# Second block's three turns worked token block by token block: first projection, transposed banks and evacuation split, ScalarE in place of VectorE for block 0

## The chip, the cores and the metric

The kernel runs on one core of one Trainium2 chip. The metric is the device time of one execution in microseconds (us). The kernel before takes 2768.85 us, the median of 3 runs (2766.33 to 2769.89). Of this kernel a difference of about 0.2% (5.5 us) can be told from none. Engines: PE is TensorE (PEld its weight loads), DVE VectorE, ACT ScalarE, POOL GpSimd, SP the engine that issues most DMAs.

## The reference

256 tokens of width 1024 pass through two layers of a first block and then through a second block. The change is in the second block:

```
for i in range(DEPTH):                         # i = 0: attention (MLA), i = 1: pooling
    hx = x * (1.0 + sc1) + sh1
    y  = mla(hx) @ w_o      or   pool_mixer(hx)
    x  = layernorm(ALPHA * x + g1 * y)
    h  = x * (1.0 + sc2) + sh2
    q  = (h @ w_q).reshape(b, l, 8, 2, 128)     # PEER: 8 heads of queries
    s  = scores of q against two sets of 128 keys; top 16 of each, top 16 of the sums
    y  = sum over the chosen experts of gate * gelu(u_e . h) * v_e
    x  = layernorm(ALPHA * x + g2 * y)
```

`pool_mixer` is a projection `h @ w_in`, a windowed mean minus the value itself per group, a grouped product, a scale and `@ w_out`. All inputs are float32. The experts are not gathered: all 128 groups of 128 are computed and weighted, most of them zero.

## The kernel before

The 256 tokens are two blocks (`tb`) of 128. `x` lies in SBUF with tokens on the partitions; a product needs `h` transposed (`hT`, features on the partitions, 8 tiles `kt` of 128 features by 256 tokens). Most products are made three times from split operands (`pe_three`, L2000): a rounded high part and the remainder of weights and of `hT` (`q_high` and `ring_r` of the weights, `PX.hh`, shown as peer_pass_high, and `h_low` of the activations). ACT rounds the high parts, DVE subtracts them to give the low ones. Each engine runs its own list in written order; semaphores tie them.

Between two stages of the second block lies what this text calls a **turn**: the end of one output product, the post-norm, the transposes, and the first projection of the next stage. There are three with a next stage: **turn A** (n=0, attention to the first expert layer, near 1001 us of the span), **turn B** (n=1, first expert layer to pooling, near 1842 us) and **turn C** (n=2, pooling to the second expert layer, near 1914 us). The last post-norm (n=3) ends the kernel.

A turn before, in order. DVE (`dve_post_norm`): for each block and each half of the features a multiply by the gate, an add and the statistics (L2409 to L2411), the aggregate (L2415); POOL turns the variance into 1/sigma (L3045, L3046), DVE normalises the block (`normalise`, L2387): block 0 after the statistics of half (1, 0), block 1 at the end. PE (`pe_transpose`) transposes block 0 as soon as it is normalised, then block 1 (L1943); a bank holds two features' tiles of both blocks, so that no bank is full before block 1 is done. Idle stretches of PE are filled with products of zeros (`pe_warm`, L514). `mod_evac` copies the four banks to `hT` with scale and shift, banks 0 and 2 by ACT (L2371), 1 and 3 by DVE (L2369). Then PE runs the first projection, plain float32, 256 columns to a matmul (query 0, L2198; z 0 in turn B, L2331), while ACT makes `PX.hh` (L2949, L3021) and the high parts of the next weights (L2626, L2610) and DVE `h_low` (L2718, L2800) and the low parts (L2617, L2603). The next projections (L2000) wait for `w_low_ready`. DVE also applies the norm's own gain and shift to `x` (L2426, L2433), which only the next post-norm needs.

In an expert layer, DVE then selects (top-16 searches L2632 to L2645, gates L2692 to L2708), with the low parts of the first experts' weights dealt in between (`EarlyLows.beside`, L2581), by which PE's `early_up` products go. PE then builds the table of weights in groups (L2264) from one-hot tiles that DVE makes.

Weights come through a ring of four SBUF slots of 1 MB. SP issues the loads in order: `used(g)` waits until PE has released the slot's previous contents. The four loads of `qk1` (queries of the second expert layer) start with ring slot 0, whose previous content is the last slot of the pooling's output product.

Of the kernel before, what the change touches and what calls it, by code (L numbers as in the profile page):

```python
# [2026 lines left out]
def pe_mla(k, pe):  # L2027
# [146 lines left out]
    pe_warm(k, pe, 0, WARM_MLA[0])  # L2174


def pe_peer(k, pe, l):
# [4 lines left out]
    def query(h):
        r = STREAM.ring(f"qk{l}", h)
        if h in SPLIT_QUERIES:
            pe.wait_ge(k.w_low_ready, query_split(l, h) + l + 1)
        else:
            pe.wait_ge(k.weights_loaded[r], STREAM.loaded(f"qk{l}", h))
        b = J.give(pe, ("q", h), l)
        for kk in range(2):
            for kt in range(KT):  # L2190
                to, w = ps[b][:, kk * S:(kk + 1) * S], slice(kk * D + kt * P, kk * D + (kt + 1) * P)
                if h in SPLIT_QUERIES:
                    m = pe_three(pe, to, (k.q_high[query_high(h)][:, w], k.ring_r[r][:, w]), (k.PX.hh[:, kt, :], k.h_low[:, kt, :]),
                                 kt == 0, kt == KT - 1)
                else:
                    if h == kk == kt % 2 == 0:
                        J.evac(pe, ("xt", kt // 2), l)
                    m = pe.matmul(to, k.ring[r][:, w], k.hT[:, kt, :], start=kt == 0, stop=kt == KT - 1)  # L2198
# [112 lines left out]
def pe_pool(k, pe):  # L2311
    J, ps = k.J4, k.psum
    pe_warm(k, pe, (k.J3.at[("g", 1)] + 1) % NBANK, WARM_LATE[0])
    pe_transpose(k, pe, J, "xt", k.x, None, k.x2_done, lambda tb: k.x2_done.at(2 + tb + 1), WARM_LATE[1])
# [1 line left out]
    for i in range(4):
        if i in SPLIT_POOL:
            pe.wait_ge(k.w_low_ready, pool_split(i) + 1)
            w = k.ring_r[STREAM.ring("pool", i)]
        else:  # L2320
            w = slot(k, pe, "pool", i)
        b = J.give(pe, ("z", i))
        for kk in range(2):
            for kt in range(KT):
                to, at = ps[b][:, kk * S:(kk + 1) * S], slice(kk * D + kt * P, kk * D + (kt + 1) * P)
                if i in SPLIT_POOL:
                    m = pe_three(pe, to, (k.q_high[i][:, at], w[:, at]), (k.PX.hh[:, kt, :], k.h_low[:, kt, :]), kt == 0, kt == KT - 1)
                else:
                    if i == kk == kt % 2 == 0:
                        J.evac(pe, ("xt", kt // 2))  # L2330
                    m = pe.matmul(to, w[:, at], k.hT[:, kt, :], start=kt == 0, stop=kt == KT - 1)  # L2331
# [1104 lines left out]
```

## Time and profile before

| | us |
|---|---|
| median of 3 runs | 2768.85 |
| the profiled execution, whole time | 2765.63 |
| its span | 2763.8 |
| what lies around the span | 1.8 |
| PE busy | 2711.2 (98%) |
| DVE busy | 2110.3 (76%) |
| ACT busy | 1245.8 (45%) |
| chain that ended last: PE, DVE | 81%, 16% |

The profile is one execution, in which an engine's busy time is the union of its instructions. Matmuls overlap each other, so PE at 98% isn't PE at its peak. The chain that ended last goes back from the last instruction, at each step to what released it. In a timeline, consecutive instructions of a kind stand as one row with a count; the brackets at a row's end give the idle time of the engine before it and who ended it.

### The profile page before, as it was taken

How to read it: one execution, taken by the hardware profiler on the slowest of the kernel's cores; microseconds unless marked ns; L12 is line 12 of the kernel's file. 1: busy time of each engine (PE TensorE's matmuls, PEld its weight loads, DVE VectorE, ACT ScalarE, POOL GpSimd, SP SyncE). 2: the span in 40 equal slices, each digit the busy share in tenths (PEclk: the TensorE clock that was granted, in tenths of full speed). 3: DMA queues.
4: the chain of work that ended last, by engine and by line, in shares of the span. 5: the costliest groups of instructions: out<-in, count | busy, mean ns of one | idle time of the engine just before them, and what ended most of it. 6: DMA issues, size and time to landing. Idle time of an engine off the chain costs nothing.

```text
span 2763.8 us, 51870 instructions
## 1 busy us (share of the span) xinstructions
PE 2711.2 (98%) x20680; PEld 2370.5 (86%) x20680; DVE 2110.3 (76%) x3795; ACT 1245.8 (45%) x1878; POOL 58.9 (2%) x86
## 2 busy tenths in 40 slices
PE   9999999999999999999999999999999999999998
PEld 7887998886998679998999998876999989999886
DVE  6867887876874669999666667775999966666777
ACT  4524554433553434454444445442445444444443
POOL 0020000020000000000000000000000000000000
PEclk9999999999999999999999999999999999999999
DMA  5315884314883235643555556664564345555664
GB/s 211 107 34 218 329 319 145 121 38 182 323 332 142 72 137 191 229 155 113 184 191 187 184 194 238 242 215 151 175 232 166 128 169 186 194 182 188 238 240 171
DMA packets 87667, 515.05 MB, mean 186 GB/s; under 512 B 10192, under 2 KB 16720, under 8 KB 30672
## 3 DMA queue, kind: packets, MB, share of 16 engines
q1 hardware_dynamic: 74256, 485.11, 48.7%
q10 hardware_dynamic: 13248, 27.63, 2.8%
q8 instruction: 119, 1.95, 0.3%
q14 instruction: 44, 0.36, 0.0%
HBM read 494.88 MB, written 17.83 MB: 186 GB/s over the span
## 4 chain that ended last, share of the span: by engine, by line
PE 81%; DVE 16%; issue 1%; ACT 1%; DMA 0%; POOL 0%; ACTq 0%; DVEq 0%; SPq 0%; POOLq 0%
PE bank L907 19%; PE bank L895 19%; PE bank L934 12%; PE bank L2000 9%; DVE ring_r L2581 4%; PE bank L2264 3%; PE bank L577 2%; PE bank L726 2%; PE bank L779 2%; PE bank L2282 1%; PE bank L655 1%; DVE sb L2645 1%; DVE sb L2636 1%; PE bank L556 1%; DVE sb L2637 1%
## 5 line engine op out<-in xcount | busy, mean ns | idle before, releaser
L2000 PE MATMUL bank<-peer_pass_high,q_high 128*128 128x256 f32 x1232 | 356.4, 289 | 1.7 <-ACT sb L2935 0.9
L2000 PE MATMUL bank<-h_low,q_high 128*128 128x256 f32 x1232 | 347.7, 282 | 0.0
L2000 PE MATMUL bank<-peer_pass_high,ring_r 128*128 128x256 f32 x1232 | 347.1, 282 | 0.0
L907 PE MATMUL bank<-peer_pass_high,peer_pass_hidden 128*128 128x512 f32 x1024 | 339.5, 393 | 0.0
L895 PE MATMUL bank<-peer_pass_high 128*128 128x256 f32 x1008 | 283.2, 281 | 0.0
L895 PE MATMUL bank<-peer_pass_high,ring_r 128*128 128x256 f32 x1008 | 282.9, 281 | 0.0
L895 PE MATMUL bank<-hT_r,peer_pass_high 128*128 128x256 f32 x1008 | 282.9, 281 | 0.0
L1013 DVE TENSOR_TENSOR ring_r<-ring,peer_pass_high 128x1024 fp32r<-128x1024 f32 x128 | 156.8, 1225 | 157.8 <-ACT peer_pass_high L1646 157.8
L2000 PEld LDWEIGHTS bank<-peer_pass_high,q_high 128*128 128x128 f32 x1232 | 233.9, 190 | 2.8 <-issue 2.2
L2000 PEld LDWEIGHTS bank<-peer_pass_high,ring_r 128*128 128x128 f32 x1232 | 233.5, 190 | 0.0
L2000 PEld LDWEIGHTS bank<-h_low,q_high 128*128 128x128 f32 x1232 | 232.8, 189 | 0.0
L1646 ACT ACTIVATE peer_pass_high<-ring 128x1024 fp32r<-128x1024 f32 x128 | 135.7, 1060 | 210.7 <-DMA ring<-in_experts 209.9
L907 PEld LDWEIGHTS bank<-peer_pass_high,peer_pass_hidden 128*128 128x128 f32 x1024 | 192.5, 188 | 38.9
L1133 ACT ACTIVATE peer_pass_high<-ring 128x1024 fp32r<-128x1024 f32 x128 | 135.5, 1060 | 164.7 <-PE bank L934 164.7
L907 PE MATMUL bank<-ring_r,peer_pass_hidden 128*128 128x512 f32 x512 | 201.2, 393 | 0.0
L1666 ACT ACTIVATE sb<-bank 128x256 f32<-128x256 f32 x192 | 73.9, 385 | 273.4 <-PE bank L895 267.9
L895 PEld LDWEIGHTS bank<-peer_pass_high 128*128 128x128 f32 x1008 | 190.0, 188 | 5.8
L895 PEld LDWEIGHTS bank<-hT_r,peer_pass_high 128*128 128x128 f32 x1008 | 190.1, 189 | 5.2
L895 PEld LDWEIGHTS bank<-peer_pass_high,ring_r 128*128 128x128 f32 x1008 | 190.0, 188 | 0.0
L907 PE MATMUL bank<-ff_high,ff_hidden 128*128 128x512 f32 x512 | 170.8, 395 | 0.8 <-DVE ff_hidden L1031 0.8
L934 PE MATMUL bank<-peer_pass_high,peer_pass_hidden 128*128 128x512 f32 x512 | 166.1, 394 | 0.9 <-DVE peer_pass_hidden L1118 0.9
L934 PE MATMUL bank<-peer_pass_high,late_hidden 128*128 128x512 f32 x512 | 165.0, 392 | 0.0
(428 smaller groups left out, 6329.4 us busy)
## 6 DMA issues: line engine op xcount, KB each, us to landing
ring<-in_experts SPq DMA_DIRECT2D x256, 1024.0 KB, 4.8
ring<-in_w SPq DMA_DIRECT2D x137, 1024.0 KB, 4.8
sb<-in_w_mod SPq DMA_DIRECT2D x48, 1024.0 KB, 6.7
sb<-spill SPq DMA_DIRECT2D x64, 256.0 KB, 4.9
spill<-sb ACTq DMA_DIRECT2D x20, 512.0 KB, 6.5
spill<-sb ACTq DMA_DIRECT2D x48, 128.0 KB, 2.3
sb<-in_ln ACTq DMA_DIRECT2D x8, 512.0 KB, 4.4
sb<-in_post ACTq DMA_DIRECT2D x4, 512.0 KB, 4.7
```

What stands on the lines that cost most here:

```text
L577: m = pe.matmul(to, w[:, cols], k.hT[:, kt, :], start=kt == 0, stop=kt == KT - 1)
L726: m = pe.matmul(ps[b][rows, h * 64:h * 64 + 64], lhsT[rows, GH * g + h, :], r, start=True, stop=True)
L895: m = pe.matmul(ps[X.banks[u]][:, 0:S], w, h[:, kt, :], start=(kt, i) == (0, 0), stop=(kt, i) == (KT - 1, 2))
L907: m = pe.matmul(ps[4 + 2 * tb + half][:, :], g[:, t], w, start=False, stop=False, skip_group_check=True)
L934: m = pe.matmul(ps[4 + 2 * tb + d][:, :], g[:, rows], w, start=False, stop=False, skip_group_check=True)
L1013: v.tensor_tensor(X.ring_r[u][:, 0:D], X.ring[u][:, 0:D], X.uh[u % 2].bitcast(F32), ALU.subtract).then_inc(X.u_split, 1)
L1133: a.activation(X.late_vh[t % 4], k.ring[r][:, half * D:(half + 1) * D], ACT.Copy).then_inc(k.late_v_high, 1)
L1646: a.activation(X.uh[u % 2], X.ring[u][:, 0:D], ACT.Copy).then_inc(X.u_high, 1)
L1666: a.activation(X.r[u % 2], k.psum[X.banks[u]][:, 0:S], func).then_inc(X.acted, 1)
L2000: m = pe.matmul(out, l, r, start=start and i == 0, stop=stop and i == 2)
L2264: m = pe.matmul(ps[g % 4][:, t * P:(t + 1) * P], k.one_hot[g % 3][:, 0, t // 2, :, t % 2], k.gate_parts[g % 2][:, i, t // 2, :, t % 2], st ...
L2581: self.v.tensor_tensor(k.ring_r[r], k.ring[r], k.q_high[early_high(s)].bitcast(F32), ALU.subtract).then_inc(k.early_low, 1)
```

## The change

The turns with n below 3 are rewritten.

- `pe_turn` replaces `pe_transpose` and the first projection. Each of the four transposed banks now holds four features' tiles of one block (`("xt", 0)` and `("xt", 1)` block 0, 2 and 3 block 1). Projection 0 is cut by block and by half of the features, 128 columns to a matmul, and the first quarter stands ahead of block 1's transposes.
- Block 0 is normalised by ACT (`act_normalise`), with a bias -mean/sigma that POOL works out in a third instruction; DVE normalises block 1 alone.
- All four banks are evacuated by ACT (`act_turn`), four instructions of 128 columns to a bank; `PX.hh` and `h_low` are made block by block.
- ACT makes the high part of the next weights (query 1, or pool slot 1) ahead of `act_normalise`; DVE makes its low part first of all after the post-norm.
- The warming products: 4 in turns A and B, ahead of the transposes; before there were 8 in A, 8 and 10 in B, 10 in C.
- `k.gate` of the expert layers moves from `hT`'s upper half to columns of `W`, and the gates are addressed as 8 x 64.
- Semaphore counts follow: `x2_first` for block 0, `hh_ready` two per turn.

```diff
-    j = [(("xt", i), both(i)) for i in range(4)]
+    j = [(("xt", i), "act") for i in range(4)]
...
+def pe_turn(k, pe, J, n, it, key, weights):
+    banks = [J.give(pe, ("xt", i), it) for i in range(4)]
+    def transposed(tb):
+        for kt in range(KT):
+            b = banks[2 * tb + kt // 4]
+            t = pe.transpose(k.psum[b][:, kt % 4 * P:(kt % 4 + 1) * P], k.x[:, tb, kt * P:(kt + 1) * P], k.c["ident"])
+            if kt % 4 == 3:
+                t.then_inc(J.filled, 1)
+    pe.wait_ge(k.x2_first, n + 1)
+    transposed(0)
+    b = J.give(pe, key, it)
+    w = weights()
+    def project(tb, half):
+        for kk in range(2):
+            for kt in range(4 * half, 4 * half + 4):
+                m = pe.matmul(k.psum[b][:, kk * S + tb * P:kk * S + (tb + 1) * P], w[:, kk * D + kt * P:kk * D + (kt + 1) * P],
+                              k.hT[:, kt, tb * P:(tb + 1) * P], start=(tb, half, kk, kt) == (0, 0, 0, 0),
+                              stop=(tb, half, kk, kt) == (1, 1, 1, KT - 1), skip_group_check=True)
+        return m
+    project(0, 0)
+    pe.wait_ge(k.x2_done.sem, k.x2_done.at(n + 1))
+    transposed(1)
+    J.evac(pe, ("xt", 1), it)
+    project(0, 1)
+    for half in range(2):
+        J.evac(pe, ("xt", 2 + half), it)
+        m = project(1, half)
+    m.then_inc(J.filled, 1)
+
+def act_normalise(k, a, n):
+    a.wait_ge(k.ln_rstd.sem, k.ln_rstd.at(2 * n + 1))
+    a.activation(k.x[:, 0, :], k.x[:, 0, :], ACT.Identity, scale=k.stat[:, 12:13], bias=k.stat[:, 0:1]).then_inc(k.x2_first, 1)
+
+def act_turn(k, a, J, it, shift, scale, high, done):
+    def evacuate(i):
+        b = J.take(a, "act", ("xt", i), it)
+        for j in range(4):
+            kt, cols = i % 2 * 4 + j, slice(i // 2 * P, (i // 2 + 1) * P)
+            m = a.activation(k.hT[:, kt, cols], k.psum[b][:, j * P:(j + 1) * P], ACT.Identity, scale=scale[:, kt:kt + 1],
+                             bias=shift[:, kt:kt + 1])
+        m.then_inc(J.read["act"], 1)
+    for tb in range(TB):
+        evacuate(2 * tb)
+        evacuate(2 * tb + 1)
+        J.evac(a, ("xt", 2 * tb + 1), it)
+        cols = slice(tb * P, (tb + 1) * P)
+        a.activation(high[:, :, cols], k.hT[:, :, cols], ACT.Copy).then_inc(done, 1)
+
+def dve_h_low(k, v, tb):
+    cols = slice(tb * P, (tb + 1) * P)
+    v.tensor_tensor(k.h_low[:, :, cols], k.hT[:, :, cols], k.PX.hh[:, :, cols].bitcast(F32), ALU.subtract).then_inc(k.w_low_ready, 1)
...
@@ dve_post_norm
-            if (tb, half) == (1, 0):
+            if (tb, half) == (1, 0) and n == 3:
                 finish(0)
...
@@ dve_peer
-    mod_evac(k, v, J, "dve", "xt", lambda kt: k.hT[:, kt, :], k.hshift[:, 2 * l, :], k.hscale[:, 2 * l, :], l)
-    dve_affine_scale(k, v, sd, J, 2 * l, l)
-    J.evac(v, ("xt", 2), l)
-    v.wait_ge(k.hh_ready, l + 1)
-    v.tensor_tensor(k.h_low, k.hT, k.PX.hh.bitcast(F32), ALU.subtract).then_inc(k.w_low_ready, 1)
     dve_query_low(k, v, l, 1)
+    v.wait_ge(k.hh_ready, 2 * l + 1)
+    dve_h_low(k, v, 0)
+    dve_affine_scale(k, v, sd, J, 2 * l, (0,), l)
+    v.wait_ge(k.hh_ready, 2 * l + 2)
+    dve_h_low(k, v, 1)
     dve_query_low(k, v, l, 2)
+    dve_affine_scale(k, v, sd, J, 2 * l, (1,), l)
     dve_affine_shift(k, v, sd)
     dve_query_low(k, v, l, 3)
...
@@ dve_pool
-    mod_evac(k, v, J, "dve", "xt", lambda kt: k.hT[:, kt, :], k.hshift[:, 1, :], k.hscale[:, 1, :])
+    dve_pool_low(k, v, 1)
+    v.wait_ge(k.w_high_ready, pool_split(1) + 1)
+    dve_h_low(k, v, 0)
     dve_diag(k, v, k.mod[:, 1, G1:G1 + 8])
...
@@ act_mla, end (and the same at the end of act_pool with 1, 1 and 2; act_pool begins with its own pair)
     act_gate_row(k, a, J, k.gbc)
+    act_query_high(k, a, 0, 1)
+    act_normalise(k, a, 0)
...
@@ pool_ln_rstd
+        if n < 3 and tb == 0:
+            sp.link(m)
+            m = p.tensor_scalar(k.stat[:, 0:1], k.mv[:, tb, 0:1], r, -1.0, ALU.mult, ALU.mult)
```

How the instructions stand. ACT in turn C, before; the first rows end the pooling stage (L2841 copies the gate row), `q_high_74` is the high part of query 1's weights, in ring slot 1:

```order
L2834 DMA sb<-in_ln 128x1024 x2
L2841 ACTIVATE sb<-bank 128x512 [waits pool_bank_filled] x2
L2371 ACTIVATE sb<-bank,sb 128x256 [waits peer_bank_filled,h_columns,x2_done]
L2371 ACTIVATE sb<-bank,sb 128x256
L2371 ACTIVATE sb<-bank,sb 128x256 [waits peer_bank_filled]
L2371 ACTIVATE sb<-bank,sb 128x256
L2949 ACTIVATE peer_pass_high<-sb 128x2048 [waits peer_bank_read_dve,peer_bank_read_act]
L2626 ACTIVATE q_high_74<-ring 128x2048 [waits weights_loaded1]
L2626 ACTIVATE q_high_75<-ring 128x2048 [waits weights_loaded2]
```

The same place of the changed kernel (L2684 is the old L2626, L1986 `act_normalise`, L1995 and L2004 `act_turn`):

```order
L2900 ACTIVATE sb<-bank 128x512 [waits pool_bank_filled] x2
L2684 ACTIVATE q_high_74<-ring 128x2048 [waits weights_loaded1]
L1986 ACTIVATE sb<-sb 128x1024 [waits ln_rstd]
L1995 ACTIVATE sb<-bank,sb 128x128 [waits peer_bank_filled,h_columns]
L1995 ACTIVATE sb<-bank,sb 128x128 x3
L1995 ACTIVATE sb<-bank,sb 128x128 [waits peer_bank_filled]
L1995 ACTIVATE sb<-bank,sb 128x128 x3
L2004 ACTIVATE peer_pass_high<-sb 128x8x128 [waits peer_bank_read_act]
L1995 ACTIVATE sb<-bank,sb 128x128 [waits peer_bank_filled]
```

The high part of query 1's weights, with its wait for the load of ring slot 1, has moved from behind the evacuation to ahead of the normalising of block 0, which itself is new on ACT.

PE in turn A, before (L514 warms, L1943 transposes, L2198 is query 0):

```order
L514 MATMUL bank<-sb 128x512 x8
L1943 MATMUL bank<-sb 128x128 [waits x2_done]
L1943 MATMUL bank<-sb 128x128 x7
L1943 MATMUL bank<-sb 128x128 [waits x2_done]
L1943 MATMUL bank<-sb 128x128 x7
L2198 MATMUL bank<-sb,ring 128x256 [waits peer_bank_read_act,weights_loaded0]
L2198 MATMUL bank<-sb,ring 128x256
L2198 MATMUL bank<-sb,ring 128x256 [waits peer_bank_read_dve]
```

And in the changed kernel (L1955 transposes, L1967 is query 0 in quarters):

```order
L514 MATMUL bank<-sb 128x512 x4
L1955 MATMUL bank<-sb 128x128 [waits x2_first]
L1955 MATMUL bank<-sb 128x128 x7
L1967 MATMUL bank<-sb,ring 128x128 [waits weights_loaded0,peer_bank_read_act]
L1967 MATMUL bank<-sb,ring 128x128 x7
L1955 MATMUL bank<-sb 128x128 [waits x2_done]
L1955 MATMUL bank<-sb 128x128 x7
L1967 MATMUL bank<-sb,ring 128x128 [waits peer_bank_read_act]
```

A quarter of query 0 has moved between the two blocks' transposes, which thereby stand behind block 0's evacuation by ACT.

## Rows read from the trace of the kernel before

**Rows 1.** The page: busy time by engine, and the chain that ended last.
```profile
PE 2711.2 (98%) x20680; PEld 2370.5 (86%) x20680; DVE 2110.3 (76%) x3795; ACT 1245.8 (45%) x1878; POOL 58.9 (2%) x86
...
PE 81%; DVE 16%; issue 1%; ACT 1%; DMA 0%; POOL 0%; ACTq 0%; DVEq 0%; SPq 0%; POOLq 0%
```

**Rows 2.** Selection: stretch, its length, busy PE, PEld, DVE, ACT, POOL, clock, DMA.
```profile
1110.00:1130.00 20.00, 20.00 (x170) 20.00 (x169) 19.79 (x76) 9.37 (x11) 0.00 (x0) 1.00 0.69 218
```

**Rows 3.** Waits: DVE 1009.5 to 1176, PE 1016.6 to 1182 (us, times, longest).
```profile
DVE sb L2443 <- DVE sb L2725: 0.2, 1, 0.2
...
PE bank L2264 <- DVE sb L2763: 1.7, 1, 1.7
```

**Rows 4.** Timeline of turn A: start, us, engine, line, instruction, count, idle before.
```profile
1000.27 0.55 POOL L3046 TENSOR_TENSOR sb<-sb 128x1 f32<-128x1 f32 x1
...
1001.76 0.80 DVE L2387 TENSOR_SCALAR sb<-sb 128x1024 f32<-128x1024 f32 x1
...
1005.81 0.81 DVE L2387 TENSOR_SCALAR sb<-sb 128x1024 f32<-128x1024 f32 x1 [0.95 <-POOL sb L3046]
...
1006.67 1.09 PE L1943 MATMUL bank<-sb 128*128 128x128 f32 x8 [2.98 <-DVE sb L2387]
1007.23 1.93 ACT L2371 ACTIVATE sb<-bank,sb 128x256 f32<-128x256 f32 x4 [28.03 <-PE bank L1943]
1007.44 1.90 DVE L2369 TENSOR_SCALAR sb<-bank,sb 128x256 f32<-128x256 f32 x4 [0.82 <-PE bank L1943]
...
1008.40 8.64 PE L2198 MATMUL bank<-sb,ring 128*128 128x256 f32 x32 [0.63 <-ACT sb L2371]
1009.26 2.35 DVE L2426 TENSOR_TENSOR sb<-sb 128x1024 f32<-128x1024 f32 x2
...
1016.68 0.47 PE L2000 MATMUL bank<-peer_pass_high,q_high 128*128 128x256 f32 x1
...
1020.52 2.29 DVE L2617 TENSOR_TENSOR ring_r<-ring,q_high 128x2048 fp32r<-128x2048 f32 x1
```

**Rows 5.** Timeline of turn B, as rows 4.
```profile
1848.52 0.64 ACTq L3017 DMA_DIRECT2D sb<-in_const  x1
...
1857.73 0.38 PE L2000 MATMUL bank<-peer_pass_high,q_high 128*128 128x256 f32 x1 [0.21 <-DVE ring_r L2603]
...
1866.68 2.28 DVE L2603 TENSOR_TENSOR ring_r<-ring,q_high 128x2048 fp32r<-128x2048 f32 x1
```

**Rows 6.** Timeline of turn C, as rows 4.
```profile
1914.02 20.39 SPq L3056 DMA_DIRECT2D ring<-in_w  x6
...
1920.23 7.14 PE L2198 MATMUL bank<-sb,ring 128*128 128x256 f32 x32 [0.63 <-ACT sb L2371]
...
1923.09 5.68 ACT L2626 ACTIVATE q_high<-ring 128x2048 fp32r<-128x2048 f32 x3
...
1927.95 0.36 PE L2000 MATMUL bank<-peer_pass_high,q_high 128*128 128x256 f32 x1 [0.57 <-issue]
...
1935.40 0.87 DVE L2632 MAX8 sb<-sb 128x8 f32<-128x128 f32 x4 [0.75 <-ACT sb L2925]
```

**Rows 7.** SP's first two loads of turn C: issues, and time to landing.
```profile
L3056 SPq DMA_DIRECT2D ring<-in_w x2: 328/380/433, 1914.0 to 1914.4; - x2
...
DMA to landing us min/median/max: 4.7/6.1/7.5
```

**Rows 8.** Groups by form: busy us, mean ns of one, idle before.
```profile
L2371 ACT ACTIVATE sb<-bank,sb 128x256 f32<-128x256 f32 x24 | 11.5, 569 | 78.3 <-PE bank L1943 78.3
L2930 ACT ACTIVATE sb<-sb 128x128 f32<-128x128 f32 x4 | 1.2, 311 | 10.3 <-DVE sb L2674 10.2
L1610 ACT ACTIVATE sb<-sb 128x1024 f32<-128x1024 f32 x3 | 3.1, 1051 | 5.4 <-DMA sb<-in_c_rows 5.4
L2209 PE MATMUL bank<-sb 128*128 128x128 f32 x128 | 16.8, 275 | 0.0
```

**Rows 9.** The same view of turn A after the transposes (0.83: granted clock).
```profile
1008.00:1018.00 10.00, 9.60 (x42) 8.40 (x43) 10.00 (x8) 9.08 (x8) 0.00 (x0) 0.83 0.15 61
```

More of the change, by code:

```diff
@@ L1844, in pool_jobs @@
 def pool_jobs():
-    j = [(("xt", i), both(i)) for i in range(4)]
+    j = [(("xt", i), "act") for i in range(4)]
     j += [(("z", i), "act") for i in range(4)]
@@ L1899, in plan_memory2 @@
     assert n.off + 4 * D <= k.mod_at + SLOT
-    k.gbc, k.lng, k.lnb, k.diag = n.take(D), n.take(D), n.take(D), n.take(8, P)
+    gbc, k.lng, k.lnb, k.diag = n.take(D), n.take(D), n.take(D), n.take(8, P)
+    k.gbc = [shaped(gbc[:, i * 512:(i + 1) * 512], 8, 64) for i in range(2)]
     k.ptmp = [k.diag.rearrange("p a b -> p (a b)")[:, i * 512:(i + 1) * 512] for i in range(2)]
@@ L2191, in query @@
                 to, w = ps[b][:, kk * S:(kk + 1) * S], slice(kk * D + kt * P, kk * D + (kt + 1) * P)
[L2192 to L2198, printed above, removed]
+                m = pe_three(pe, to, (k.q_high[query_high(h)][:, w], k.ring_r[r][:, w]), (k.PX.hh[:, kt, :], k.h_low[:, kt, :]),
+                             kt == 0, kt == KT - 1)
                 rel.pay(m) if kt == 0 else None
@@ L2312, in pe_pool @@
     J, ps = k.J4, k.psum
-    pe_warm(k, pe, (k.J3.at[("g", 1)] + 1) % NBANK, WARM_LATE[0])
-    pe_transpose(k, pe, J, "xt", k.x, None, k.x2_done, lambda tb: k.x2_done.at(2 + tb + 1), WARM_LATE[1])
+    pe_warm(k, pe, (k.J3.at[("g", 1)] + 1) % NBANK, WARM_LATE)
     rel = Release(k)
[L2316 to L2321, printed above, removed]
+    pe_turn(k, pe, J, 1, None, ("z", 0), lambda: slot(k, pe, "pool", 0))
+    rel.owe()
+    for i in SPLIT_POOL:
+        pe.wait_ge(k.w_low_ready, pool_low(i))
+        w = k.ring_r[STREAM.ring("pool", i)]
         b = J.give(pe, ("z", i))
@@ L2325, in pe_pool @@
                 to, at = ps[b][:, kk * S:(kk + 1) * S], slice(kk * D + kt * P, kk * D + (kt + 1) * P)
[L2326 to L2331, printed above, removed]
+                m = pe_three(pe, to, (k.q_high[i - 1][:, at], w[:, at]), (k.PX.hh[:, kt, :], k.h_low[:, kt, :]), kt == 0, kt == KT - 1)
                 rel.pay(m) if kt == 0 else None
@@ L2609, in act_pool_high @@
     a.wait_ge(k.weights_loaded[r], STREAM.loaded("pool", i))
-    a.activation(k.q_high[i], k.ring[r], ACT.Copy).then_inc(k.w_high_ready, 1)
+    a.activation(k.q_high[i - 1], k.ring[r], ACT.Copy).then_inc(k.w_high_ready, 1)
 def dve_query_low(k, v, l, i):
@@ L2840, in act_gate_row @@
         b = J.take(a, "act", ("g", i), it)
-        a.activation(gate[:, i * 512:(i + 1) * 512], k.psum[b][:, :], ACT.Copy).then_inc(J.read["act"], 1)
+        a.activation(gate[i], shaped(k.psum[b][:, :], 8, 64), ACT.Copy).then_inc(J.read["act"], 1)
 def act_keys(k, a, l):
@@ L2945, in early_up @@
                         k.early[:, n - 3:n + 1, :].rearrange("p a b -> p (a b)")).then_inc(k.early_out, 16)
[L2947 to L2950 removed]
+    for i in (2, 3):
         act_query_high(k, a, l, i)
@@ L3242, in build @@
         k.PX.late_gl = k.PX.gl + [spare[:, (2 + i) * S:(3 + i) * S] for i in range(2)]
-        k.gate = k.sb[:, k.hT_at + 4 * S:k.hT_at + KT * S]
+        k.gate = [k.W[:, 8 * i:8 * i + 8, 0:EXP_SLOTS] for i in range(2)]
         k.FF = Pass(k, ctx, nc, "ff", FF_SLOTS, k.ff_at, k.ff_hi, FF_RING, k.J1.at[("h2", 0)] % NBANK)
```

89 lines of the change are left out of this document (42 added, 47 removed).

## The prediction

> **What bounds the kernel now.** I read the page first: PE is busy in 98% of the span, and the chain that ended last is PE for 81% and DVE for 16% [rows 1]. So a turn matters only by when PE can go on, and where DVE's 16% lie. The stretches of the selection phase answer the second: from 1110 to 1130 PE is busy for 20.00 of 20 us and DVE for 19.79 [rows 2]. The waits complete it: from the end of turn A's evacuation to the end of the selection DVE waits 0.2 us in all, and PE 1.7 us at the first group of gates, for DVE [rows 3]. Both are full, but DVE ends last. So a turn ahead of an expert layer (A and C) is worth what it gives DVE, read at the last low part of the turn, where nothing of DVE's list can be moved: L2617 at 1020.52 in A [rows 4]. PE's gain beyond that is lost in waits for the experts' low parts. Last come the timelines of the turns [rows 4 to 6] and the landings of the loads [rows 7].
>
> **Turn A, step by step.** DVE drops the normalising of block 0 (0.80 us, about 0.7 with its overlap), so block 1's normalise moves from 1005.81 to 1005.1 and ends at 1005.9 [rows 4]. POOL's power ends at 1000.82 [rows 4]; with a third small instruction ACT can begin at 1001.25, and 128x1024 takes ACT 1.05 [rows 8]: block 0 is ready at 1002.3, before the former 1002.6. PE transposes it (1.09 for eight [rows 4]); bank 0 is full at 1003.0, ACT starts at 1003.15. What one ACT instruction of 128 columns costs isn't in the trace. Four of 256 take 1.93 with 0.569 the last, so they start 0.45 apart [rows 4, 8]. The bounds are 0.45 above (nothing saved by half the columns) and 0.25 below (0.311 for a 128x128 without a column bias [rows 8], less overlap). I take 0.35, near the middle. Eight then take 2.9. The high part of a block (half of 1.9) is 1.05.
>
> ACT: block 0 to 1006.05, its high part to 1007.2. PE: quarter (0, 0) from 1004.8. A 128-column float32 matmul counts two instructions, and the scores' 16 runs of eight take 1.05 each with 0.275 the last, so 0.111 apart [rows 8]; a quarter is 16 of them, 1.8. All four are 7.1, what 32 of 256 columns take at full clock (7.14 [rows 6]): the split costs PE nothing. Quarter (0, 0) ends at 1006.6, then come block 1's transposes, which could have started at 1006.0. ACT evacuates block 1 from 1007.4 to 1010.3, its high part is there at 1011.45. PE ends the last quarter at 1013.1 and can begin query 1, before at 1016.68 [rows 4]: 3.5 earlier.
>
> DVE: low part 1 from 1006.0 to 1008.25 (2.29 each [rows 4]), `h_low` 0 (1.2) and one scaling (1.2, half of L2426's 2.35 [rows 4]) to 1010.6. Here 0.9 of waiting is new, for ACT's high part; `h_low` 1 to 1012.7; again 0.65 of waiting, because ACT makes high part 2 only now (to 1013.3); low part 2, a scaling, two shifts, and low part 3 ends at 1021.3, before at 1022.8 (1020.52 + 2.29). DVE is relieved of 0.7, of 1.90 for the evacuation and of the wait of 0.82 [rows 4], but waits 1.6 for ACT, which now carries all. **A: -1.5**, bounds 0 (ACT at 0.45) and -3.5 (all of PE's gain counts).
>
> **Turn B.** The same, with pool slot 1 landed well ahead, since the last experts' loads end earlier. On ACT, two DMA issues (one of them 0.64, L3017 [rows 5]) now stand between block 1 and high part 2, about 1.0 in all. DVE's low part 3, which projection 3 waits for, was done at 1868.96 [rows 5]; the same sum gives 1867.25, and the pooling adds behind it fill DVE. **B: -1.7**, bounds 0 and -3.1 (PE's own: projection 1 at 1854.6 for 1857.73 [rows 5]).
>
> **Turn C.** Here one step changes sign. ACT's list has the high part of query 1 ahead of block 0's normalise, and it needs ring slot 1. SP starts all four loads of `qk1` only at 1914.02, when the output product has released its last slot; the first lands after 4.7, the second, issued at 1914.4, after 7.5: 1921.9 [rows 6, 7]. Before, ACT came to it at 1923.09 and found it there [rows 6]. Now ACT stands still from the gate row on; behind it are the normalise, all evacuations and both high parts, PE's transposes wait for the normalise, and DVE for both. Slot 1 lands at 1921.9, the high part ends at 1923.85, block 0 is normalised at 1924.9. Before, block 0 was normalised about when the output product ended, 1914. From there the sum of turn A, with nothing to hide it: ACT starts on bank 0 at 1925.75, ends block 0's high part at 1929.8, takes bank 2 at 1929.95, and ends block 1's high part at 1934.0; `h_low` 1 at 1935.25; PE begins query 1 at 1935.5, before at 1927.95 [rows 6]: +7.6. DVE: high part 2 is made by 1935.85, low part 2 to 1938.1, scaling and shifts to 1941.5, low part 3 to 1943.7, and the first search starts at 1943.9, before at 1935.40 [rows 6]: +8.5.
>
> To this comes the clock. In turn A PE waits 2.98 and 0.63 [rows 4], and then is granted 0.83 over 1008 to 1018 (the lower level, 1.2 GHz, for a third of it) [rows 9]: query 0 takes 8.64 for 7.14 [rows 4, 6]. In turn C PE now has nothing for 11 us. The lower level for the transposes alone costs 0.5 of the chain, for the first quarter too 2.1; with nothing lowered 0. I take 1.5, what query 0 lost in A. **C: +10.0**, bounds +7.6 and +12.5 (with ACT at 0.45).
>
> The Trainium skill (TensorE: Matmul & The Clock Gate, Part 1: The HAM clock gate) has the slow clock as the default, which only activity lifts; the trace agrees [rows 9]. By that rule turn C resumes at 1.2 GHz for certain; by a rule that the clock depends on the matmuls alone it wouldn't, and C were +8.5. A and B lose warming products too, but PE's gaps there shrink to about 1 us, and I set 0.
>
> At nothing: `k.gate`'s strided address (as many elements), the keys' DMA 1.4 later (needed by query 1 at 1013, behind two loads already in flight), and POOL's third instruction, which only block 0 waits for (0.3, included).
>
> **Sum:** -1.5 - 1.7 + 10.0 = +6.8. The profiled execution took 2765.63 (span 2763.8 and 1.8 around it), so 2772.4 by its own measure. It lies 3.2 under the median of the runs, 2768.85, so that what is timed should read 2775.6.
>
> **The rivals.**
> 1. *PE decides, not DVE.* Then A is -3.5, B -3.1, C +7.6 and 1.5 of clock: +2.5, 2771.4. For it: the chain is PE's in 81%, and where PE waits it waits for 1.7 only [rows 1, 3]. Against it: DVE has no gap in which to take up its part [rows 2, 3].
> 2. *Faster: ACT isn't held.* Were slot 1 there by the time ACT reaches it, C would be like A and the wait of 0.75 at L2632 [rows 6] would go too, -2.3: the sum is -5.5, 2763.3. It decides if the second load lands before about 1915. For it is only that SP might issue slot 1 earlier; against it that SP's list is unchanged and its first issue of the four is at 1914.02 [rows 6]. A partial case: both loads share the DMA engines and land together at 4.7, which makes slot 1 2.8 earlier: +4.0, 2772.9. The Trainium skill (DMA: Bandwidth & Descriptors, Queues, rings and completion order) says that completion isn't in the order of issue; here the two land 3.2 apart in order [rows 7]. By the page's rule alone the sum would be +4.0 or +6.8.
> 3. *The clock falls in all three turns.* The new PE lists alternate short work and waits of 1 us with fewer warming products. 1.5 more in A and in B, and 1 more in C: +10.8, 2779.7. For it: rows 9, after 3 us of waiting; against it: no waits of that length are left in A and B.
>
> **Numbers.** Chances: forecast 0.70, rival 1 0.13, rival 2 0.08 (with its partial case), rival 3 0.09. A difference under 0.2% (5.5 us) can't be told from none. The forecast's own range goes from 2771.5 (+2.7: gains near their bounds, no clock) to 2780 (+11); within it about a quarter lies under +5.5. Slower: 0.70 x 0.74 + 0.09 = 0.61; faster 0.05, half of rival 2 and a little; same 0.34. The range for 8 in 10 takes in most of rival 1 and of rival 3: 2769 to 2781.
>
> **What would show it.** In the changed profile: in turn C the normalise L1986 waits behind L2684, and L2684 for DMA into the ring, over 30 us of idle ACT ended by in_w; L1955 there starts near 1925 less what A and B gave (3.2), that is near 1922; PE idle for about 11 us ahead of it and the granted clock under 1 right after. In A the search starts 1.5 earlier, with two DVE waits for ACT (0.9 and 0.65), and PE waits more often for low parts. In B projection 3 waits for L2661's low part. I am wrong if L2684 in turn C is done before the output product's end, if the 128-column evacuations start 0.25 or 0.45 apart, or if the selection ends earlier than DVE's share allows.

## The result

| | median us | n | ratio to before, 95% interval |
|---|---|---|---|
| before | 2768.16 | 19 | |
| changed | 2773.5 | 19 | 1.002 [1.0013, 1.0027] |

The change makes the kernel 5.3 us slower, just under the 5.5 that were called the smallest telling difference; forecast were +6.8 and 2775.6. The interval lies above 1, so the loss is clear of the spread, though small. The profiled execution has a span of 2769.4 for 2763.8. Of all executions behind the ratios below, three were left out of them as far above the rest (2970 to 9953 us: one of experiment 8, two of the kernel before beside experiments 5 to 8); the medians include them.

The page of the changed kernel, as in [rows 1]:

```profile
PE 2705.3 (98%) x20739; PEld 2371.3 (86%) x20748; DVE 2103.7 (76%) x3783; ACT 1260.9 (46%) x1920; POOL 59.7 (2%) x89
...
PE 79%; DVE 17%; issue 2%; ACT 2%; DMA 1%; POOL 0%; DVEq 0%; ACTq 0%; SPq 0%; POOLq 0%
```

PE is busy 5.9 less and the end is 5.6 later: PE stands still somewhere. ACT and DMA, which had 1% and 0% of the chain, now have 2% and 1%.

To price each turn by itself I measure from the first `BATCH_NORM_AGGREGATE` of a turn to the first search (`MAX8`) of the expert layer behind it, or in turn B to the aggregate of turn C. So what happens outside the turns drops out.

| profile | A | B | C |
|---|---|---|---|
| before | 25.00 | 70.33 | 23.94 |
| changed | 23.37 | 67.35 | 33.86 |
| difference | -1.63 | -2.98 | +9.92 |
| forecast | -1.5 | -1.7 | +10.0 |

The three sum to +5.3, 1.5 less than the forecast's +6.8, and 1.3 of that lies in turn B. From C's first search to the last aggregate it is 822.2 in both.

Timeline of turn C of the changed kernel (columns as [rows 6]), all engines:

```profile
1907.12 0.21 DVE L2464 BATCH_NORM_AGGREGATE sb<-sb 128x2 f32<-128x12 f32 x1
...
1909.68 35.98 SPq L3118 DMA_DIRECT2D ring<-in_w  x7
...
1917.21 1.91 ACT L2684 ACTIVATE q_high<-ring 128x2048 fp32r<-128x2048 f32 x1 [35.35 <-DMA ring<-in_w]
1919.03 1.23 ACT L1986 ACTIVATE sb<-sb 128x1024 f32<-128x1024 f32 x1
...
1920.31 1.97 PE L1955 MATMUL bank<-sb 128*128 128x128 f32 x8 [10.63 <-ACT sb L1986]
1921.52 2.90 ACT L1995 ACTIVATE sb<-bank,sb 128x128 f32<-128x128 f32 x8 [1.26 <-PE bank L1955]
...
1923.07 3.55 PE L1967 MATMUL bank<-sb,ring 128*128 128x128 f32 x16 [0.80 <-ACT sb L1995]
...
1926.46 1.04 PE L1955 MATMUL bank<-sb 128*128 128x128 f32 x8
1927.09 2.90 ACT L1995 ACTIVATE sb<-bank,sb 128x128 f32<-128x128 f32 x8 [1.59 <-PE bank L1955]
...
1931.11 1.22 DVE L2010 TENSOR_TENSOR h_low<-sb,peer_pass_high 128x1024 fp32r<-128x1024 f32 x1 [3.22 <-ACT peer_pass_high L2004]
1932.91 2.29 DVE L2675 TENSOR_TENSOR ring_r<-ring,q_high 128x2048 fp32r<-128x2048 f32 x1 [0.58 <-ACT q_high L2684]
...
1938.77 2.29 DVE L2675 TENSOR_TENSOR ring_r<-ring,q_high 128x2048 fp32r<-128x2048 f32 x1
1940.98 0.86 DVE L2690 MAX8 sb<-sb 128x8 f32<-128x128 f32 x4
```

The reader is to see one row first: ACT was idle for 35.35 us and was released by the load into the ring, at 1917.21, 7.5 after SP's first issue. The chain that ended last passes through it: the second of SP's loads, from 1910.05, for 7.14 us, then this high part, the normalise and the transposes. Behind it come the normalise, PE (idle for 10.63) and DVE. Between the last low part and the search DVE has no gap, so its list still decides. The clock there, by stretches (columns as [rows 2]):

```profile
1914.00:1918.00 4.00, 0.00 (x0) 0.00 (x0) 0.00 (x0) 0.79 (x1) 0.00 (x0) 0.50 1.01 422
1918.00:1922.00 4.00, 1.69 (x8) 1.56 (x8) 1.72 (x1) 2.73 (x4) 0.00 (x0) 0.50 0.81 342
1922.00:1926.00 4.00, 3.20 (x15) 2.93 (x14) 1.04 (x2) 3.47 (x8) 0.00 (x0) 0.50 0.00 0
1926.00:1930.00 4.00, 4.00 (x36) 4.00 (x36) 1.89 (x2) 2.90 (x8) 0.00 (x0) 0.97 0.00 0
```

It fell while PE had nothing to do, and stayed at 0.50 through the transposes and the first quarter of query 0.

Turn A of the changed kernel answers to [rows 4]:

```profile
1002.64 1.24 ACT L1986 ACTIVATE sb<-sb 128x1024 f32<-128x1024 f32 x1 [4.78 <-POOL sb L3107]
...
1004.68 2.90 ACT L1995 ACTIVATE sb<-bank,sb 128x128 f32<-128x128 f32 x8 [0.81 <-PE bank L1955]
...
1006.24 2.05 PE L1967 MATMUL bank<-sb,ring 128*128 128x128 f32 x16 [1.22 <-ACT sb L1995]
...
1012.78 1.22 DVE L2010 TENSOR_TENSOR h_low<-sb,peer_pass_high 128x1024 fp32r<-128x1024 f32 x1 [0.88 <-ACT peer_pass_high L2004]
...
1014.58 2.29 DVE L2675 TENSOR_TENSOR ring_r<-ring,q_high 128x2048 fp32r<-128x2048 f32 x1 [0.58 <-ACT q_high L2684]
```

Eight small evacuations take 2.90 and DVE's two new waits for ACT are 0.88 and 0.58.

### The profile page after: what moved, and what is told of

Read it like the earlier page. It is cut to its first block, busy times and chain, and to the rows that moved or that the text cites. A ratio compares the mean times of both kernels' runs of the same rounds, so it can differ in the third digit from the quotient of the medians.

```text
span 2769.4 us, 52027 instructions
## 1 busy us (share of the span) xinstructions
PE 2705.3 (98%) x20739; PEld 2371.3 (86%) x20748; DVE 2103.7 (76%) x3783; ACT 1260.9 (46%) x1920; POOL 59.7 (2%) x89
## 4 chain that ended last, share of the span: by engine, by line
PE 79%; DVE 17%; issue 2%; ACT 2%; DMA 1%; POOL 0%; DVEq 0%; ACTq 0%; SPq 0%; POOLq 0%
PE bank L907 19%; PE bank L895 19%; PE bank L934 12%; PE bank L2064 8%; DVE ring_r L2631 3%; PE bank L2320 3%; PE bank L577 2%; PE bank L726 2%; PE bank L779 2%; PE bank L2338 1%; PE bank L2051 1%; DVE sb L2703 1%; DVE sb L2694 1%; PE bank L655 1%; DVE sb L2695 1%
## 5 line engine op out<-in xcount | busy, mean ns | idle before, releaser
L934 PE MATMUL bank<-peer_pass_high,peer_pass_hidden 128*128 128x512 f32 x512 | 166.0, 394 | 0.0
L934 PE MATMUL bank<-peer_pass_high,late_hidden 128*128 128x512 f32 x512 | 165.1, 392 | 0.0
```

The costliest lines, as they stand in the source:

```text
L934: m = pe.matmul(ps[4 + 2 * tb + d][:, :], g[:, rows], w, start=False, stop=False, skip_group_check=True)
```

## The experiments

There are twelve. Medians are of 10 to 12 executions each (experiment 12 is one execution), beside the kernel before in the same session; the three sessions had 2766.40 (experiments 1 to 4), 2767.74 (5 to 8) and 2767.08 (9 to 11) for it. Times of different sessions are compared by their distance from it; the changed kernel's is 5.3. The turns in the profile of each:

| | A | B | C | median | ratio to before, 95% interval |
|---|---|---|---|---|---|
| changed | 23.37 | 67.35 | 33.86 | 2773.50 | 1.0020 [1.0013, 1.0027] |
| 1 high part late in C | 25.02* | 67.36 | 27.56 | 2767.31 | 1.0001 [0.9992, 1.0010] |
| 2 slot order 1, 2, 0, 3 | 23.39 | 69.00* | 25.33 | 2765.35 | 0.9992 [0.9982, 1.0003] |
| 3 and transposes first | 25.02* | 67.36 | 24.97 | 2761.66 | 0.9979 [0.9970, 0.9988] |
| 4 C warmed | 25.03* | 67.35 | 33.55 | 2772.32 | 1.0018 [1.0009, 1.0027] |
| 5 less DVE in A | 20.97 | 67.36 | 34.56 | 2770.59 | 1.0011 [1.0002, 1.0020] |
| 6 less PE in A | 23.39 | 67.36 | 34.53 | 2774.50 | 1.0022 [1.0014, 1.0031] |
| 7 hold in the kernel before | 25.68 | 70.35 | 30.41 | 2773.63 | 1.0023 [1.0013, 1.0032] |
| 8 gaps warmed | 23.38 | 67.35 | 33.71 | 2772.04 | 1.0014 [1.0002, 1.0026] |
| 9 as 3, again | 23.39 | 67.35 | 24.95 | 2761.40 | 0.9978 [0.9967, 0.9989] |
| 10 slots and warming | 23.38 | 67.37 | 22.37 | 2758.76 | 0.9972 [0.9961, 0.9983] |
| 11 and DVE's waits filled | 22.12 | 67.35 | 22.26 | 2758.57 | 0.9968 [0.9956, 0.9980] |
| 12 kernel before, again | 24.99 | 70.48 | 23.94 | 2764.44 (one) | |

A star marks a turn of the new form in which the clock fell in the first quarter of projection 0, which then took 3.5 to 3.7 for 2.05. The profiles differ most where no turn is: turn A's first aggregate comes at 996.1 to 1005.0, so a difference of a few us between two profiled spans says less than the turns do.

**Is it the hold?** Experiment 1 moves the one instruction, and DVE's low part that follows from it, in turn C alone.

```diff
-    act_query_high(k, a, 1, 1)          # end of act_pool, ahead of act_normalise(k, a, 2)
...
-    for i in (2, 3):                    # act_peer, behind act_turn
+    for i in (2, 3) if l == 0 else (1, 2, 3):
...
-    dve_query_low(k, v, l, 1)           # DVE: in layer 1 behind dve_h_low(k, v, 1)
```

> The changed kernel, but in turn C alone ACT makes query 1's high part behind act_turn, with queries 2 and 3, instead of ahead of act_normalise (DVE's low part 1 stands behind h_low 1). Theory (the high part's wait for ring slot 1 holds ACT, and with it everything of the turn): the 35 us of idle ACT ended by in_w are gone from before the normalise; block 0 is normalised as soon as POOL's power is there, about when the output product ends, and PE now waits for slot 0, which lands 4.7 after its issue; turn C loses about 2 against the kernel before instead of 9.9, the whole is 7 to 8.5 faster than the changed kernel. Rival (the new order of PE's list and the eight small evacuations cost turn C most of its 9.9): the normalise comes early, but the first search of turn C stays over 6 later than before, and the whole within 3 of the changed kernel.

```profile
1907.80 1.24 ACT L1986 ACTIVATE sb<-sb 128x1024 f32<-128x1024 f32 x1 [26.91 <-POOL sb L3109]
...
1913.91 2.80 PE L1967 MATMUL bank<-sb,ring 128*128 128x128 f32 x16 [3.72 <-DMA ring<-in_w]
...
1916.50 1.91 PE L1955 MATMUL bank<-sb 128*128 128x128 f32 x8
```

Turn C lost 3.6 instead of 9.9, and the kernel is level with the one before: 4.4 less than the changed kernel, where 7 to 8.5 were expected. By turn C the hold is 6.3 of the 9.9. My 2 was too small by 1.6: PE's new wait of 3.72 for slot 0 also lets the clock fall (quarter 2.80 for 2.05, transposes 1.91 for 1.04), and block 1's transposes stand behind that quarter. Turn A of this profile had its own fall (25.02).

**The same from the other side.** Experiment 2 leaves the lists of all engines that compute and changes only SP's order of loads.

```diff
-        for pos in range(0 if seg == "mla" else RING):
+        for pos in () if seg == "mla" else (1, 2, 0, 3) if seg == "qk1" else range(RING):
```

> The changed kernel, but SP issues the four loads of qk1 in the order slot 1, 2, 0, 3; slots 1 and 2 were released earlier in the pooling, slots 0 and 3 only at the end of the output product. The other engines' lists are unchanged. Theory (only the landing of slot 1 holds ACT): the high part of query 1 is made well before the output product ends, ACT's wait for in_w goes, and turn C now waits for slot 0, 4.7 after its issue: first search of turn C 8 earlier than in the changed kernel, the whole 8 less. Partial rival (slot 0 shares the queue with two loads that are still in flight and lands later): 5 to 6 less. Rival (ACT is held by something else): nothing changes.

```profile
1912.92 1.24 ACT L1986 ACTIVATE sb<-sb 128x1024 f32<-128x1024 f32 x1 [12.81 <-POOL sb L3107]
...
1918.76 3.04 PE L1967 MATMUL bank<-sb,ring 128*128 128x128 f32 x16 [3.45 <-DMA ring<-in_w]
```

ACT now waits for POOL, not for the load, and turn C is 8.5 shorter, as expected. The median is 1.1 under the kernel before, an interval that takes in 1, and 6.4 under the changed kernel, where 8 were expected; turn B had a fall of the clock in this profile (69.00). C is still 1.4 over the old one, since PE waits 3.45 for slot 0. No list of an engine that computes was changed, so the wait for slot 1, with what it brings on, is shown as the cause of 8.5 of the 9.9. Slot 1 itself was free long before: here ACT has it at 1898.20, 13 us ahead of the turn's first aggregate. In the changed kernel its load only stood in SP's list behind the one for slot 0.

**The hold put into the kernel before** (experiment 7):

```diff
     J = k.J3                            # act_peer of the kernel before
+    if l == 1:
+        act_query_high(k, a, l, 1)
     a.wait_ge(k.x2_done.sem, k.x2_done.at(4 * l + 2))
...
-    for i in (1, 2, 3):
+    for i in (1, 2, 3) if l == 0 else (2, 3):
```

> The kernel before, with one instruction moved: in turn C ACT makes the high part of query 1 ahead of the evacuation of the transposed banks, not behind it. Theory (the hold by the load of slot 1 is what costs turn C, whatever the rest of the turn is): ACT starts the evacuation when slot 1 has landed and its high part is made, near 1923.8 for 1919.06 (4.8 later); query 0 begins 4.8 later; DVE gets low part 1 about 2 earlier in exchange, so that the first search is 3 to 5 later and the whole 3 to 5 more than before. Rival (turn C loses by the new order of PE's and DVE's lists): no change.

```profile
1922.48 1.91 ACT L2626 ACTIVATE q_high<-ring 128x2048 fp32r<-128x2048 f32 x1 [35.70 <-DMA ring<-in_w]
1924.29 1.91 ACT L2371 ACTIVATE sb<-bank,sb 128x256 f32<-128x256 f32 x4
1925.44 9.79 PE L2198 MATMUL bank<-sb,ring 128*128 128x256 f32 x32 [5.28 <-ACT sb L2371]
```

One moved instruction costs the old kernel 5.9 in the median and 6.5 in turn C, where 3 to 5 were expected. The evacuation starts 4.66 later from the aggregate, as expected; what lies above is the clock, since query 0 took 9.79 for 7.14 and the search there waits 2.90 for the scores.

**The clock's share of turn C.** Experiment 4 puts 44 warming products ahead of turn C's transposes.

```diff
 def pe_peer(k, pe, l):
     J, c, ps = k.J3, k.c, k.psum
+    if l == 1:
+        pe_warm(k, pe, 3, 44)
```

> The changed kernel with 44 warming products on PE at the start of turn C, ahead of the block 0 transposes, which cover most of its 10.6 us of idle time there. Theory (of turn C's +9.9 some 1.5 to 2 are the clock, 8.4 the hold): the granted clock stays at 1.00 from 1913 to 1927, query 0's quarters take 1.8 to 2.05 for two of 3.55 to 1.97, and turn C is 1.5 to 2 shorter. Rival (ACT and DVE set the end there, whatever PE's clock): the clock stays up but the first search comes no earlier. Neither expects the 8.

```profile
1926.03 1.09 PE L1955 MATMUL bank<-sb 128*128 128x128 f32 x8 [1.13 <-ACT sb L1986]
...
1928.35 3.59 PE L1967 MATMUL bank<-sb,ring 128*128 128x128 f32 x16 [1.22 <-ACT sb L1995]
```

A miss. The transposes ran fast, but the clock fell in the first quarter again (granted 0.79 from 1928 to 1929, then 0.50). C took 33.55, against 33.86, 34.56 and 34.53 where it wasn't warmed: 0.3 to 1.0 shorter. So in this one profile the gaps of 1.13 and 1.22 around the transposes were enough for a fall. The clock's share can still be read from the changed kernel: ACT started 1.21 after PE, in turn A 0.75, and the quarter took 3.55 for 2.05, together 2.0. In experiments 5 and 6 the lower level lasted longer (quarter 3.78, block 1's transposes 1.91 and 1.68 for 1.04) and C was 0.7 longer, so the share is 2.0 to 2.7.

**What decides turn A.** Experiment 5 relieves DVE by leaving out the norm's shift of `x`, experiment 6 PE by leaving out a third of query 2's products; each gives up that part of the computation.

```diff
-    dve_affine_shift(k, v, sd)          # experiment 5, dve_peer
+    if l == 1:
+        dve_affine_shift(k, v, sd)
+    else:
+        sd.settle()
```

```diff
+                if (l, h) == (0, 2):    # experiment 6, pe_peer, query(h)
+                    pe.matmul(to, k.q_high[query_high(h)][:, w], k.PX.hh[:, kt, :], start=kt == 0, stop=False)
+                    m = pe.matmul(to, k.ring_r[r][:, w], k.PX.hh[:, kt, :], start=False, stop=kt == KT - 1)
...
```

> The changed kernel; in turn A DVE leaves out the two additions of the norm's shift to x (2.36 of DVE between low parts 2 and 3), so that part of the computation is missing. Theory (an expert turn is worth what it gives DVE): low part 3, the first search and the first group of gates all come 2.3 earlier, counted from the turn's first aggregate, and the whole is 2.3 less. Rival (PE decides): the first search comes earlier, PE's first group of gates doesn't, and the whole is within 0.5 of the changed kernel.

> The changed kernel; query 2 of the first expert layer leaves out one of its three partial products (low activations by high weights), 16 matmuls and about 1.9 of PE's time. Theory (DVE decides): PE only waits 1.9 more further on, and the time is that of the changed kernel. Rival (PE decides turn A): 1.9 less.

Without DVE's 2.36 turn A is 2.40 shorter, and the first group of gates, which came 157.2 after the search in the changed kernel, still comes 157.2 after it (157.2 in the kernel before as well). Without PE's 1.9 turn A stays at 23.39, and so does that distance. PE's waits of the selection phase (us in all, times, longest), first of the changed kernel, then of experiment 6:

```profile
PE bank L2320 <- DVE sb L2822: 1.7, 1, 1.7
PE bank L2064 <- DVE ring_r L2675: 1.1, 1, 1.1
```

```profile
PE bank L2064 <- DVE ring_r L2679: 3.0, 1, 3.0
PE bank L2324 <- DVE sb L2826: 1.7, 1, 1.7
```

The 1.9 went one for one into the wait for low part 3. The medians go the same way: 2.9 above before for experiment 5, so 2.5 less than the changed kernel, and 6.8 for experiment 6, no less.

**The clock in turns A and B.** Three of the first five profiles of the new form showed A at 25.0, with the clock down in the first quarter.

```diff
-WARM_BEGIN, WARM_MIX, WARM_LATE, WARM_FF, WARM_MLA = 24, 21, 4, 26, 4
+WARM_BEGIN, WARM_MIX, WARM_LATE, WARM_FF, WARM_MLA = 24, 21, 8, 26, 8
...
     transposed(0)
+    pe_warm(k, pe, banks[3], 5)
```

> The changed kernel with PE's gaps of turns A and B filled: 8 for 4 warming products ahead of block 0's transposes, and 5 new ones behind them, where PE waits 1.2 for ACT's first evacuation (the same 5 in turn C). In three of five profiles of kernels with the new turn A the clock fell in its first quarter of query 0 (3.68 for 2.05), and turn A then took 25.0 from the first aggregate to the first search, as before the change; where it didn't fall, 23.4. Theory (the gaps let the clock fall, and the first quarter ahead of block 1's transposes makes it cost): the clock stays at 1.00 in A and B, A takes 23.4, and the median is 0.5 to 2.5 less than the changed kernel's. Rival (the clock falls by chance, or in the cover of the waits): A as before in as many executions, no difference.

A and B were undisturbed here and in the other two kernels with this warming (experiments 10 and 11), so in 3 of 3; without it the clock fell in A in 3 of 8 profiles and in B in 1 of 8. Three profiles are few: with a chance of 3 in 8 each, three without a fall would come in a quarter of all cases. The median is 1.0 less than the changed kernel's, each by its distance from the kernel before, and the intervals overlap: the profiles point to the theory, neither they nor the times settle it. In turn C of experiment 8 the five products ran at 0.50 themselves:

```profile
1924.92 2.34 PE L514 MATMUL bank<-sb 128*128 128x512 bf16 x5
1927.05 2.18 PE L1968 MATMUL bank<-sb,ring 128*128 128x128 f32 x16
```

The quarter took 2.18 for 3.55, but began 1.13 later, and turn C was only 0.15 shorter than in the changed kernel.

How a fall enters turn A is in two rows of experiment 1:

```profile
1003.56 3.68 PE L1967 MATMUL bank<-sb,ring 128*128 128x128 f32 x16 [1.22 <-ACT sb L1995]
...
1011.74 1.23 DVE L2010 TENSOR_TENSOR h_low<-sb,peer_pass_high 128x1024 fp32r<-128x1024 f32 x1 [2.52 <-ACT peer_pass_high L2004]
```

The quarter stands ahead of block 1's transposes, so its 1.63 more is passed on to ACT and makes DVE's wait 2.52 for 0.88. The last run asks whether the kernel before paid for its own fall [rows 9]:

> The kernel before, profiled once more, for its turn A. Theory (DVE's list decides turn A there, with a cover for PE that only an early fall of the clock uses up): 25.0 from the first aggregate to the first search, whether the clock falls in query 0 or not. Rival (those 25.0 were long because of the fall of the clock near 1008): without a fall about 23.4, as after the change, and the change gave turn A nothing.

```profile
1007.01 8.83 PE L2198 MATMUL bank<-sb,ring 128*128 128x256 f32 x32 [0.63 <-ACT sb L2371]
...
1023.23 0.87 DVE L2632 MAX8 sb<-sb 128x8 f32<-128x128 f32 x4
```

A took 24.99, but the clock fell again, as in all three profiles of the old form, so the case without a fall wasn't seen. What speaks for the theory: query 0 took 8.64 and 8.83, the search came at 25.00 and 24.99, and DVE's only waits there for another engine (0.95 and 0.82) lie before the fall. In experiment 7 it fell already in the transposes (query 0 9.25 for the old turn A), and then A took 25.68, with a wait of 0.30 for the scores ahead of the search: only there did the fall reach the search.

**A version that beats both.** Experiment 3 adds to the slot order that turn C transposes block 1 ahead of the first quarter.

```diff
     transposed(0)
+    if n == 2:
+        pe.wait_ge(k.x2_done.sem, k.x2_done.at(n + 1))
+        transposed(1)
...
     project(0, 0)
-    pe.wait_ge(k.x2_done.sem, k.x2_done.at(n + 1))
-    transposed(1)
+    if n < 2:
+        pe.wait_ge(k.x2_done.sem, k.x2_done.at(n + 1))
+        transposed(1)
```

> As the one before (slot order 1, 2, 0, 3), and in turn C PE transposes block 1 before the first quarter of query 0, since it must wait for slot 0 there anyhow. If the wait for slot 0 is then the last thing ahead of block 1's evacuation, this gives 1.5 to 2 more than slot order alone: 9.5 to 10 less than the changed kernel, 4 to 5 less than the kernel before. Rival (slot 0 lands before the first quarter could start): no more than slot order alone.

> The kernel with slot order 1, 2, 0, 3 and block 1's transposes first in turn C, again, beside the next two. As measured: 4.7 less than the kernel before, ratio 0.998.

Measured: 4.7 less than before, and 5.7 in the repetition. Turn C gained only 0.4 over experiment 2, where 1.5 to 2 were expected, because query 0 stayed at the lower clock for long, 9.18 for 7.1, and the search now waits for the scores:

```profile
1930.94 0.88 DVE L2694 MAX8 sb<-sb 128x8 f32<-128x128 f32 x4 [3.02 <-ACT sb L2990]
```

That row is of experiment 9; experiment 3 has 3.03. PE no longer waits for slot 0 at all, so on this point the rival was right. Yet the median fell by 3.7. The profiles of experiments 2 and 3 don't explain that: the one had its fall in turn B, the other in A. The two intervals overlap, so some of it can be spread. Experiment 10 adds the warming of the last section, with 12 products in turn C:

> The one before it plus the warming: 8 for 4 products ahead of turns A and B, 5 behind block 0's transposes there, and 12 behind them in turn C, where PE waits 2.77 for block 1's normalise and then ran all of query 0 at the lower clock (9.18 for 7.1). Theory (in turn C PE is now the one that ends last, since the first search waits 3.0 for the scores): query 0 takes 7.1 to 7.5, the first search of C comes 1.5 to 2 earlier, A takes 23.4 in every execution; 2 to 3 less than slot order and transposes alone. Rival (the clock falls all the same): no difference.

Turn C of experiment 9, then of experiment 10, by stretches of 4 us:

```profile
1909.00:1913.00 4.00, 1.24 (x9) 1.00 (x10) 2.86 (x6) 3.27 (x9) 0.74 (x2) 0.83 0.85 297
1913.00:1917.00 4.00, 4.00 (x20) 4.00 (x20) 4.00 (x3) 3.71 (x10) 0.00 (x0) 0.50 0.55 229
1917.00:1921.00 4.00, 4.00 (x32) 4.00 (x31) 2.84 (x3) 4.00 (x3) 0.00 (x0) 0.82 0.00 0
```

```profile
1905.00:1909.00 4.00, 3.56 (x21) 2.00 (x20) 2.70 (x5) 3.19 (x9) 0.74 (x2) 1.00 0.70 238
1909.00:1913.00 4.00, 3.82 (x33) 3.46 (x32) 3.91 (x4) 3.97 (x10) 0.00 (x0) 1.00 0.71 293
1913.00:1917.00 4.00, 4.00 (x39) 4.00 (x38) 3.22 (x3) 3.97 (x4) 0.00 (x0) 1.00 0.00 0
```

Full clock throughout and C 2.6 shorter in the profile, where 1.5 to 2 were expected; A and B are those of experiment 9. The median is 2.6 less too, though the intervals overlap. Here warming pays, since the scores end last in this turn C and hardly a gap is left between the products and the work. Experiment 11 moves one DVE instruction:

```diff
+    dve_affine_scale(k, v, sd, J, 2 * l, (1,), l)
     v.wait_ge(k.hh_ready, 2 * l + 2)
     dve_h_low(k, v, 1)
     dve_query_low(k, v, l, 2)
-    dve_affine_scale(k, v, sd, J, 2 * l, (1,), l)
```

> As the one before, and in both expert turns DVE applies the norm's gain to block 1 ahead of its wait for block 1's high part, not behind low part 2: the waits of 0.88 and 0.58 in turn A are filled. Theory (DVE decides turn A): low part 3 and the first search come 1.2 earlier in A, 1.2 less in the whole; turn C, where the scores decide, gains nothing. Rival (PE decides): no difference, or 0.3 more, because query 1 gets its second low half 0.3 later.

```profile
1008.06 1.22 DVE L2015 TENSOR_TENSOR h_low<-sb,peer_pass_high 128x1024 fp32r<-128x1024 f32 x1
1009.70 2.29 DVE L2680 TENSOR_TENSOR ring_r<-ring,q_high 128x2048 fp32r<-128x2048 f32 x1 [0.42 <-ACT q_high L2689]
```

The wait of 0.88 is gone, turn A is 1.26 shorter in the profile as expected; the median moved by 0.2 where 1.2 were expected, so the times show no gain. Against the kernel before experiment 11 gains 8.5 us (0.9968 [0.9956, 0.9980]).

## Why the prediction was right, step by step

- **Turn A, right** (-1.63 for -1.5). ACT's 2.90 for eight instructions of 128 columns and both waits (0.88 and 0.58 for 0.9 and 0.65) came as worked out; the normalise on ACT took 1.24 for 1.05, without effect on the end. That DVE decides was shown by experiments 5 and 6. Left out was that the gain isn't firm: a fall of the clock in the new first quarter takes all of it, which rival 3 had for A in mechanism and size (1.5; measured 1.63), but for every execution. It was seen in 3 of 8.
- **Turn B, the mis-sized term** (-2.98 for -1.7; PE's own bound was -3.1). I put "two DMA issues" at about 1.0 between block 1 and high part 2. They cost ACT nothing that shows: they ran beside the last `PX.hh`, and the high part followed at once.

```profile
1850.48 1.06 ACT L2004 ACTIVATE peer_pass_high<-sb 128x1024 fp32r<-128x1024 f32 x1
1850.49 0.33 ACTq L2905 DMA_DIRECT2D sb<-in_w  x1
1850.86 0.45 ACTq L3078 DMA_DIRECT2D sb<-in_const  x1
1851.45 1.90 ACT L2668 ACTIVATE q_high<-ring 128x2048 fp32r<-128x2048 f32 x1
```

  So low part 3 began 22.71 after the aggregate, before 25.55 [rows 5]: 2.84 earlier. PE now waits 0.19 for it at the first product of projection 3 (1864.82), where it didn't wait before, so DVE decides B by a hair, as forecast. This rests on rows; no run varied turn B alone.
- **Turn C, right** (+9.92 for +10.0). The hold by slot 1 has four witnesses: the row of 35.35 us, and experiments 1, 2 and 7. Rival 2, that the load is there in time, isn't the case of the changed kernel. Experiment 2 makes it so, and C was +1.4, where the rival had -2.3: it left out that PE then waits 3.45 for slot 0. The first of the four loads landed 5.0 after its issue, and slot 1 released ACT 7.5 after that issue; the partial case (both at 4.7) did not come. Within the term the hold was nearer to 8.0 and the clock to 2.0 than to 8.5 and 1.5; the two errors cancel, so that the term's closeness (0.1) is in part luck. The rule of the Trainium skill that the slow clock is the default and only activity lifts it (TensorE: Matmul & The Clock Gate, Part 1: The HAM clock gate) agrees with this trace: after 10.6 us without work PE resumed at 0.50, that is 1.2 GHz.
- **Rival 1** (PE decides in A) fell with experiment 6. The prediction counted 1.7 us of PE's waits in the selection phase; the view has 0.6 more, for ACT (L2935), which changes nothing here.
- **Outside the turns** two profiles differ by amounts that no term had: +1.36 ahead of turn A, and -1.09 between A's first search and turn B. The second is a PE wait of about 1 at L934 for DVE's L1118. It is there in all three profiles of the old form and, of the new form, in experiment 6 alone, and in experiment 4 in the second layer instead. Whether the change has a part in it stays open; in an execution it is worth about 1.1.

## What to carry to other kernels

When an instruction moves to an earlier place on its engine, look at what it waits for, not at what it costs: a 1.9 us conversion moved ahead of the normalise cost 8, since its load stood in SP's list behind one whose slot the stage before releases last. The repair may lie elsewhere, in the order in which the queue loads slots that are free. And work placed between a short PE gap and the thing others wait for carries the clock's fall into their path (1.63 in turn A). Behind it the fall seems to have cost nothing in the kernel before, which no run without a fall confirms; where the scores end last, as in experiment 9, up to 2.6.

## What the runs showed of the hardware that was not expected

- A PE gap need not be long. In one profile, behind 44 warming products, gaps of 1.13 and 1.22 us around eight transposes were followed by a fall in the quarter behind them (3.59 us); with products in both gaps of turns A and B the first quarter took 2.05 in all three profiles. Between the last product and the quarter PE did nothing but transposes there, so whether the gaps alone bring the fall, or transposes don't hold the clock as other products do, isn't shown.
- Warming products issued while the clock is down run at the lower level themselves: five took 2.34 us in turn C of experiment 8, 1.24 in turn A of experiment 11. The quarter behind them was 1.37 shorter and began 1.13 later.
- DMA issues of 0.33 and 0.45 us on ACT's queue took nothing from the ACTIVATE that was running (1.06 us, as without them), and the next began as it ended.
